# Seven block products for pair 10 and for six more second units, with the conditioning laid out anew

## The chip, the cores and the metric

One core of a Trainium2 chip runs the whole program in one launch. The metric is device time in microseconds (us), the median of several runs. A profiled execution has its own time, and a span from its first to its last instruction.

## The reference, cut to what matters

Two transformer blocks in float32 on 512 tokens of width 1024. Between the mixers stand five gated feed-forward networks, called network 0 to 4 here (four of hidden width 2816 in the first block, one of 2816 in the second):

```
def _swiglu(h, w_in, w_out):
    a, b = jnp.split(h @ w_in, 2, axis=-1)
    return (jax.nn.silu(a) * b) @ w_out

x = x + 0.5 * _swiglu(_rmsnorm(x, ffn_norm[layer, 0]), ffn_w_in[layer, 0], ffn_w_out[layer, 0])
...
x = x + g2 * swiglu(modulate(rms_norm(x, norm2_gain[layer]), sh2, sc2), w_ffn_in[layer], w_ffn_out[layer])
...
mod = jax.nn.silu(c) @ w_ada[layer] + b_ada[layer]
```

The last line, the conditioning, is a product of one vector (two with the context's) with a 1024 x 6144 matrix. The second block needs its result, the kernel computes it on VectorE beside networks 0, 1 and 2.

## The kernel before, in words

**Units.** All large weights come in units of 128 x 2048 float32 (1 MB): 256 output features of 1024 inputs. SyncE loads unit after unit into two buffers by turns (RAW), each load released by the low part of the unit two before. ScalarE rounds the block to its high part (WH, `split`, L604), as soon as the unit two before, which used the same buffer, is done on TensorE. VectorE takes the low part (WL = RAW - WH, L1456). A plain unit is 8 x 2 x 3 matmuls of 512 columns (high by high, high by low, low by high; `three`, L2603 to L2605).

**A network.** 22 input units in 11 pairs (pair i is units 2i and 2i+1), then 12 output units in four groups of three (8, 8 and 6 of the 22 hidden rows, so the third unit has 36 matmuls). The first unit of a pair gives the gate part, which is scaled by the norm (RINV; networks 0 to 3, called late in the code) and goes through silu on ScalarE; the second gives the factor, and `gated` (L1732, L1736) multiplies both into GF. `high_g` on ScalarE (L819) and `low_g` on VectorE (L1811) split GF into GHI and GLO, on which the output units work. GHI lies on the memory of the token sums TH and TL and of the weight sums SH and SL.

**Seven products.** In the pairs listed in SEVEN the first unit, and in those in SEVEN_B the second too, is computed by a Strassen-like scheme: the 2 x 2 blocks of weights and tokens are combined so that seven block products of 12 matmuls of 256 columns each do for eight. For it VectorE makes four sums of weight blocks in RAW (`raw_sums`, L1760 to L1770), ScalarE their high parts (L792), VectorE their low parts (`sums_low`, L1777); after the unit VectorE joins the seven results from PSUM (`joined`, L1794 to L1799 for a first unit, L1791 to L1799 for a second) with one result that ScalarE copied out (`first_product`, L812). `scaled_seven` (L1806) is the scaling. On TensorE `seven` waits for `q_raw` and, as a first unit, for `a_ready` (network 4: `silu_ready`) of the pair before, as a second for `g_mul`; its third, fourth and fifth products wait for the low parts of one sum each, the sixth for `w_lo`.

**Order by hand.** VectorE's order in pair i of `ffn_seven`, networks 0 to 2, is: gating of pair i-1; the low part of unit 2i+1 (or sums and their low parts, if by seven); joining of unit 2i; raw sums of unit 2i+2; scaling of pair i; low sums of unit 2i+2; half a conditioning block, if ADA_IN has the pair. In network 0 the low parts of the token sums (L1752) stand in pair 2, ahead of the low sums. Each engine takes its work in this order.

**Conditioning.** 24 blocks, 8 per network, each in two halves of 512 KB that GpSimd loads into one buffer (ADAW). A half is eight operations of 128 x 256 on VectorE (L1612, L1615), an odd one is followed by a transpose into PSUM and a reduction (L1621, L1623; bank 7 in the pairs, bank 3 in the output units). ADA_IN gives the halves per pair (before and after the low sums), ADA_OUT those per output unit, where `beside(c)` places them behind the low part of unit c+1. Of the 16 halves 8 stand in pairs 2 to 9 and 8 in output units 1, 2, 4, 5, 7, 8, 9 and 10.

**The end of the input.** Pair 10 is plain in all networks; GHI is written from unit 19's end on (`visit_done` >= u0 + 20), three pairs of GLO ahead of unit 20's scaling, four behind it.

```
def conditioned(count, bank):
...
                if i in SEVEN[n]:
                    joined(i)
                else:
                    scaled(i)
                if i + 1 in SEVEN[n]:
                    raw_sums(i + 1)
```

Of the kernel before, what the change touches and what calls it, by code (L numbers as in the profile page):

```python
# [42 lines left out]
FFN_IN, FFN_OUT = 22, 12  # L43
# [92 lines left out]

N_LATE = 6

SEVEN = {0: range(3, 10), 1: range(2, 10), 2: range(2, 10), 3: range(2, 10), 4: range(2, 10)}

SEVEN_B = {3: (3, 5, 7, 9), 4: (2, 3, 5, 6, 8, 9)}

ADA_IN = {2: (0, 1), 3: (0, 1), 4: (0, 1), 5: (0, 1), 6: (0, 1), 7: (0, 1), 8: (0, 1), 9: (0, 1)}
ADA_OUT = {1: 1, 2: 1, 4: 1, 5: 1, 7: 1, 8: 1, 9: 1, 10: 1}

ONCE_DVE = ("zeros", "fold_ready", "mlb_in", "c_ready", "c_lo", "mod_ready", "ml_rows", "ml_bl")
ONCE_ACT = ("cond_ready", "fx_const", "c_hi", "sb_const", "crms", "ml_bh")
# [5 lines left out]
def build(nc, A):  # L153
    ctx = ExitStack()
    with ctx:
# [441 lines left out]
        def _(act):  # L597
# [171 lines left out]
            def ffn_seven(n, shift=None, lead=None, rest=None, aside=None):  # L769
                u0, m_, name = U_FFN[n], N_NORM[FFN_NORM[n]], FFN_NORM[n]  # L770
                late = m_ < N_LATE

                def silu(i):
                    if not late and i in SEVEN[n]:
                        act.wait_ge(*q_posts(n, i, 4))
                    elif not late:
                        act.wait_ge(T["g_mul"].sem, 22 * n + 2 * i)
                        act.wait_ge(T["visit_done"].sem, u0 + 2 * i + 1)
                    for m in range(2):
                        if late:  # L780
                            act.wait_ge(T["a_ready"].sem, 22 * n + 2 * i + m + 1)
                        x = SIL7 if i in SEVEN[n] else SIL
                        act.activation(x[:, m, :], x[:, m, :] if late or i in SEVEN[n] else PS[:, m, :], ACT.Silu).then_inc(*T["silu_ready"].up())

                def sums_high(i, s=0):

                    u, before = u0 + 2 * i + s, units_upto(n, i, s)
                    for q in range(4):
                        act.wait_ge(*q_sums(n, i, q, s))
                        if before and q < 3:  # L790
                            act.wait_ge(T["q_prod"].sem, 4 * before - 2 + q)
                        act.activation(sum_high(u, q), sum_raw(u, q), ACT.Copy).then_inc(*T["q_hi"].up())  # L792

                def tokens_whole():

                    for t in range(KT):
                        last = act.activation(HG[:, t, :], XT[:, t, :], ACT.Copy, scale=gain_of(name, t))
                    last.then_inc(*T["q_hi"].up())

                def tokens_high(t0, t1):  # L800

                    for t in range(t0, t1):
                        act.wait_ge(T["q_sum"].sem, q_sums(n, SEVEN[n][0], t - 4)[1])
                        act.activation(TH[:, t, :, :], TF[:, t, :, :], ACT.Copy).then_inc(*T["q_hi"].up())

                def first_product(i, s=0):

                    before = units_upto(n, i, s)
                    act.wait_ge(*q_prods(n, i, 0, s))
                    if before:  # L810
                        act.wait_ge(T["q_post"].sem, 4 * before - 3)
                    act.activation(WB[:, 0, :] if s else WK[:, 0, :], PS[:, first_bank(s), 0:SC], ACT.Copy).then_inc(*T["q_copy"].up())  # L812

                def high_g(p0, p1):
                    for p in range(p0, p1):
                        act.wait_ge(T["g_mul"].sem, 22 * n + 2 * p + 2)
                        if p == 0:
                            act.wait_ge(T["visit_done"].sem, u0 + 20)
                        act.activation(GHI[:, 2 * p:2 * p + 2, :], GF[:, 2 * p:2 * p + 2, :], ACT.Copy).then_inc(*T["gh_ready"].up())  # L819

                def beside(c):
                    if c == 0:
                        high_g(8, 11)
                    if aside:
                        aside(c)

                if not late:
                    first_parts(n, shift)
                    T["q_hi"].up()
                elif lead:  # L830
                    lead()
                    split(u0 + 2)
                else:
                    split(u0 + 1)
                if late and not lead:
                    tokens_whole()
                if late:
                    inverse(m_)
                if rest:
                    rest()  # L840
                if not lead:
                    split(u0 + 2)
                silu(0)
                if not lead:
                    tokens_high(0, 4)
                for i in range(1, FFN_IN // 2):
                    split(u0 + 2 * i + 1)
                    if lead and i == 1:
                        tokens_whole()
                    if i in SEVEN[n]:  # L850
                        first_product(i)
                    if i in SEVEN_B.get(n, ()):
                        sums_high(i, 1)
                    if i == FFN_IN // 2 - 1:
                        high_g(0, 4)
                    split(u0 + 2 * i + 2)
                    if i in SEVEN_B.get(n, ()):
                        first_product(i, 1)
                    if not late:
                        silu(i)  # L860
                    if i + 1 in SEVEN[n]:
                        sums_high(i + 1)
                    if late:
                        silu(i)
                    if lead and i == 1:
                        tokens_high(0, 4)
                high_g(4, 8)
                residual(RES[f"ffn{n}"], u0 + FFN_IN, 3, False, ("mix0", "ffn2", "mix1", None, None)[n], beside)

            def residual(r, u0, chunks, loop, then=None, aside=None, ahead=0):  # L870
# [580 lines left out]
        def _(dve):  # L1451
# [248 lines left out]
            def ffn_seven(n, gain=None, shift=None, scale=0.5, lead=None, rest=None, aside=None):  # L1700
# [113 lines left out]
                carries = n < N_ADA // ADA_PER  # L1814
                taken = [2 * ADA_PER * n]

                def conditioned(count, bank):

                    for j in range(carries * count):
                        u, h = taken[0] // 2, taken[0] % 2  # L1820
                        conditioning(u, h)
                        if h:
                            if bank < 4:
                                dve.wait_ge(T["g_mul"].sem, 22 * n + 22)
                            turned_sums(u - ADA_PER * n + 1, ADA_PER * n - 1, bank)
                        taken[0] += 1

                def beside(c):
                    if c < 2:
                        low_g(7 + 3 * c, 10 + c)  # L1830
                    conditioned(ADA_OUT.get(c, 0), 3)
                    if carries and c == 11:
                        modulation(n, 3)
                    if aside:
                        aside(c)
# [18 lines left out]
                for i in range(1, FFN_IN // 2):  # L1854
                    gated(i - 1)
                    if i in SEVEN_B.get(n, ()):
                        raw_sums(i, 1)
                        sums_low(i, 1)
                    else:
                        split(u0 + 2 * i + 1)  # L1860
                    if i == 1 and not lead:
                        token_lows(0, 4)
                    if i == FFN_IN // 2 - 1:
                        low_g(0, 3)
                    conditioned(ADA_IN.get(i, (0, 0))[0], 7)
                    if i in SEVEN[n]:
                        joined(i)
                    else:
                        scaled(i)
                    if i + 1 in SEVEN[n]:  # L1870
                        raw_sums(i + 1)
                    if i in SEVEN[n]:
                        scaled_seven(i)
                    if i == 2 and lead:
                        token_lows(0, 4)
                    if i + 1 in SEVEN[n]:
                        sums_low(i + 1)
                    else:
                        split(u0 + 2 * i + 2)
                    if i == 1 and lead:  # L1880
                        token_sums()
                    conditioned(ADA_IN.get(i, (0, 0))[1], 7)
                low_g(3, 7)
                gated(FFN_IN // 2 - 1)
                residual(RES[f"ffn{n}"], u0 + FFN_IN, 3, False, scale, ("mix0", "ffn2", "mix1", None, None)[n], beside)

            def residual(r, u0, chunks, loop, scale, then=None, aside=None, ahead=0):
# [712 lines left out]
        def _(pe):  # L2600
# [193 lines left out]
            def ffn_seven(n, aside=None):  # L2794
# [9 lines left out]
                for i in range(FFN_IN // 2):  # L2804
                    for s in range(2):
# [14 lines left out]
                        feature_major(u % 2, HH, HL, (2 * s, 2 * s + 1), ready=8 * m_ if i + s == 0 else None).then_inc(*T["visit_done"].up())  # L2820
                        if i + s == 0:
                            norm(m_)
                residual(RES[f"ffn{n}"], u0 + FFN_IN, FFN_CHUNKS, GHI, GLO, False, 22 * n, aside=beside)
                if carries:
                    pe.wait_ge(T["ada_mod"].sem, n + 1)
# [660 lines left out]
```

## Time and profile before

| | |
|---|---|
| median of 3 runs | 2769.15 us (2769.1 to 2770.93) |
| profiled execution | 2770.69 us |
| its span | 2769.0 us |
| TensorE busy | 2748.1 us, 99% |
| VectorE busy | 1859.5 us, 67% |
| ScalarE busy | 1168.3 us, 42% |
| granted TensorE clock, mean | 0.998 |

Busy time of TensorE is the time with a matmul under way; matmuls overlap in the records, so the mean of one (389 ns for 512 columns) is more than its share of the time. The clock is of full speed, 2.4 GHz, through all stages with which the change has to do. In timeline rows the first number is a start in us from the span's begin, the second the time to the end of the last instruction merged into the row.

### The profile page before, as it was taken

Reading aid. Unit: us, or ns where it says so; the run is one execution under the profiler, and the core shown is the slowest. Engines: PE = TensorE matmul, PEld = TensorE weight load, DVE = VectorE, ACT = ScalarE, POOL = GpSimd, SP = SyncE. Lnnn points to the kernel's source line nnn. Section 1 sums busy time; section 2 is a strip of 40 time slices with the busy share of each in tenths; the row PEclk is TensorE's granted clock in tenths of the full one; section 3 lists DMA queues with packets and bytes.
Section 4 is the critical chain, followed back from the end, with each engine's and each line's share of the span. In section 5 each row is a group of like instructions: output and inputs, shape, how many; then the busy total and the mean of one; then the engine's idle time right before and its main releaser. Section 6 shows DMA issues by size and latency. Waiting matters only on the chain. (4 is left out here: it accounts for less than half of the span.)

```text
span 2769.0 us, 37283 instructions
## 1 busy us (share of the span) xinstructions
PE 2748.1 (99%) x15352; PEld 2367.4 (85%) x15352; DVE 1859.5 (67%) x2563; ACT 1168.3 (42%) x1406; POOL 39.3 (1%) x77
## 2 busy tenths in 40 slices
PE   9999999999999999999999999999999999999998
PEld 7898887789988899888877899888898988899988
DVE  6997666468885688865665688835555543688743
ACT  5333237453342433423555544424443432444422
POOL 0000000000000000000000000000000000000000
PEclk9999999999999999999999999999999999999999
DMA  4333441123334333334111233224321122223332
GB/s 163 114 131 129 134 139 63 46 99 122 124 120 145 129 108 123 129 134 127 59 49 61 107 107 108 102 97 157 109 80 67 47 77 100 71 103 107 107 107 76
DMA packets 69106, 289.22 MB, mean 104 GB/s; under 512 B 7680, under 2 KB 30336, under 8 KB 40528
## 3 DMA queue, kind: packets, MB, share of 16 engines
q1 hardware_dynamic: 60480, 257.18, 26.9%
q0 software_dynamic: 8032, 29.37, 3.3%
q8 instruction: 121, 1.98, 0.3%
q10 hardware_dynamic: 432, 0.36, 0.0%
q14 instruction: 41, 0.34, 0.0%
HBM read 284.78 MB, written 2.10 MB: 104 GB/s over the span
## 5 line engine op out<-in xcount | busy, mean ns | idle before, releaser
L604 ACT ACTIVATE sb_WH<-sb_RAW 128x2048 fp32r<-128x2048 f32 x238 | 455.5, 1914 | 783.0 <-PE PS L2605 780.0
L2603 PE MATMUL PS<-sb_HH,sb_WH 128*128 128x512 f32 (+1 forms) x2100 | 757.8, 361 | 5.2 <-DVE sb_WL L1456 1.8
L2604 PE MATMUL PS<-sb_HL,sb_WH 128*128 128x512 f32 (+1 forms) x2100 | 751.8, 358 | 0.0
L2605 PE MATMUL PS<-sb_HH,sb_WL 128*128 128x512 f32 (+1 forms) x2100 | 751.5, 358 | 0.0
L1456 DVE TENSOR_TENSOR sb_WL<-sb_RAW,sb_WH 128x2048 fp32r<-128x2048 f32 x190 | 434.7, 2288 | 347.7 <-ACT sb_WH L604 347.7
L2603 PEld LDWEIGHTS PS<-sb_HH,sb_WH 128*128 128x128 f32 x2100 | 396.7, 189 | 69.5 <-issue 3.3
L2604 PEld LDWEIGHTS PS<-sb_HL,sb_WH 128*128 128x128 f32 x2100 | 396.9, 189 | 58.2 <-issue 1.4
L2605 PEld LDWEIGHTS PS<-sb_HH,sb_WL 128*128 128x128 f32 x2100 | 396.6, 189 | 58.4
L2603 PE MATMUL PS<-glh_GHI,sb_WH 128*128 128x512 f32 (+1 forms) x924 | 350.8, 380 | 0.0
L2605 PE MATMUL PS<-glh_GHI,sb_WL 128*128 128x512 f32 (+1 forms) x924 | 350.2, 379 | 0.0
L2604 PE MATMUL PS<-glh_GLO,sb_WH 128*128 128x512 f32 (+1 forms) x924 | 350.1, 379 | 0.0
L2605 PEld LDWEIGHTS PS<-glh_GHI,sb_WL 128*128 128x128 f32 x924 | 173.8, 188 | 32.8
L2603 PEld LDWEIGHTS PS<-glh_GHI,sb_WH 128*128 128x128 f32 x924 | 173.8, 188 | 32.7
L2604 PEld LDWEIGHTS PS<-glh_GLO,sb_WH 128*128 128x128 f32 x924 | 173.8, 188 | 32.6
L2603 PE MATMUL PS<-sv_TH,sv_SH 128*128 128x256 f32 x588 | 166.4, 283 | 0.0
L2604 PE MATMUL PS<-sv_TL,sv_SH 128*128 128x256 f32 x588 | 166.4, 283 | 0.0
L2605 PE MATMUL PS<-sv_TH,sv_SL 128*128 128x256 f32 x588 | 166.4, 283 | 0.0
L792 ACT ACTIVATE sv_SH<-sb_RAW 128x512 fp32r<-128x512 f32 x147 | 93.1, 634 | 155.0 <-DVE sb_RAW L1763 130.2
L1615 DVE SCALAR_TENSOR_TENSOR ff_ACC<-ff_ADAW,sb_CS,ff_ACC 128x256 f32<-128x256 f32 x336 | 137.1, 479 | 2.8 <-DMA ff_ADAW<-in_w_ada 2.8
L2603 PE MATMUL PS<-sb_WH,sb_HH 128*128 128x256 f32 x448 | 132.2, 295 | 0.0
L2604 PE MATMUL PS<-sb_WL,sb_HH 128*128 128x256 f32 x448 | 127.0, 284 | 0.0
L2605 PE MATMUL PS<-sb_WH,sb_HL 128*128 128x256 f32 x448 | 127.0, 284 | 0.0
(455 smaller groups left out, 4011.7 us busy)
## 6 DMA issues: line engine op xcount, KB each, us to landing
sb_RAW<-in_weights SPq DMA_DIRECT2D x221, 1024.0 KB, 4.9
ff_ADAW<-in_w_ada POOLq DMA_DIRECT2D x48, 512.0 KB, 3.9
sb_RAW<-in_weights SPq DMA_DIRECT2D x39, 512.0 KB, 5.0
out_t<-sb_XT SPq DMA_DIRECT2D x8, 256.0 KB, 2.4
sb_XT<-in_x SPq DMA_DIRECT2D x3, 512.0 KB, 8.5
sb_RAW<-in_weights SPq DMA_DIRECT2D x4, 256.0 KB, 3.5
b_CT<-in_ctx POOLq DMA_DIRECT2D x1, 1024.0 KB, 7.2
hy_BD<-in_c_gates POOLq DMA_DIRECT2D x1, 512.0 KB, 3.5
```

Source lines behind the costliest of these rows:

```text
L604: act.activation(WH[slot][:, :], RAW[slot][:, :], ACT.Copy).then_inc(*T["w_hi"].up())
L792: act.activation(sum_high(u, q), sum_raw(u, q), ACT.Copy).then_inc(*T["q_hi"].up())
L1456: dve.tensor_tensor(WL[slot][:, :], RAW[slot][:, :], f32(WH[slot][:, :]), ALU.subtract).then_inc(*T["w_lo"].up())
L1615: ins = dve.scalar_tensor_tensor(ACC[:, j, :], w, c, ACC[:, j, :], ALU.mult, ALU.add)
L2603: pe.matmul(out, wh, xh, start=start, stop=False)
L2604: pe.matmul(out, wh, xl, start=False, stop=False)
L2605: return pe.matmul(out, wl, xh, start=False, stop=stop)
```

## The change

Pair 10 goes into SEVEN in all five networks. Pairs 3 and 7 of networks 0, 1 and 2 go into SEVEN_B. Conditioning leaves pairs 3 and 7 and joins output units 3 and 6. As pair 10's products read the token sums, GHI is written from unit 20's end on; all eight high parts of pairs 0 to 7 follow one another on ScalarE behind unit 22's, four of their low parts stand on VectorE between the low part of unit 22 and pair 10's scaling and four behind it. Gating of pair 10 moves behind the low part of output unit 1. TensorE waits ahead of the output units for pair 10's joining, since they write its banks.

```diff
-SEVEN = {0: range(3, 10), 1: range(2, 10), 2: range(2, 10), 3: range(2, 10), 4: range(2, 10)}
-
-SEVEN_B = {3: (3, 5, 7, 9), 4: (2, 3, 5, 6, 8, 9)}
-
-ADA_IN = {2: (0, 1), 3: (0, 1), 4: (0, 1), 5: (0, 1), 6: (0, 1), 7: (0, 1), 8: (0, 1), 9: (0, 1)}
-ADA_OUT = {1: 1, 2: 1, 4: 1, 5: 1, 7: 1, 8: 1, 9: 1, 10: 1}
+SEVEN = {0: range(3, 11), 1: range(2, 11), 2: range(2, 11), 3: range(2, 11), 4: range(2, 11)}
+
+SEVEN_B = {0: (3, 7), 1: (3, 7), 2: (3, 7), 3: (3, 5, 7, 9), 4: (2, 3, 5, 6, 8, 9)}
+
+ADA_IN = {2: (0, 1), 4: (0, 1), 5: (0, 1), 6: (0, 1), 8: (0, 1), 9: (0, 1)}
+ADA_OUT = {1: 1, 2: 1, 3: 1, 4: 1, 5: 1, 6: 1, 7: 1, 8: 1, 9: 1, 10: 1}
...
                         if p == 0:
-                            act.wait_ge(T["visit_done"].sem, u0 + 20)
+                            act.wait_ge(T["visit_done"].sem, u0 + 21)
...
-                    if i == FFN_IN // 2 - 1:
-                        high_g(0, 4)
                     split(u0 + 2 * i + 2)
                     if i in SEVEN_B.get(n, ()):
                         first_product(i, 1)
+                    if i == FFN_IN // 2 - 1:
+                        high_g(0, 8)
...
-                high_g(4, 8)
                 residual(RES[f"ffn{n}"], u0 + FFN_IN, 3, False, ("mix0", "ffn2", "mix1", None, None)[n], beside)
...
-                def conditioned(count, bank):
+                def conditioned(count, bank, done):
...
                         if h:
-                            if bank < 4:
-                                dve.wait_ge(T["g_mul"].sem, 22 * n + 22)
+                            dve.wait_ge(T["g_mul"].sem, 22 * n + 2 * done)
                             turned_sums(u - ADA_PER * n + 1, ADA_PER * n - 1, bank)
...
                 def beside(c):
-                    if c < 2:
-                        low_g(7 + 3 * c, 10 + c)
-                    conditioned(ADA_OUT.get(c, 0), 3)
+                    if c == 0:
+                        gated(FFN_IN // 2 - 1)
+                        low_g(8, 10)
+                    elif c == 1:
+                        low_g(10, 11)
+                    conditioned(ADA_OUT.get(c, 0), 3, 11)
...
-                    if i == FFN_IN // 2 - 1:
-                        low_g(0, 3)
-                    conditioned(ADA_IN.get(i, (0, 0))[0], 7)
+                    conditioned(ADA_IN.get(i, (0, 0))[0], 7, i)
                     if i in SEVEN[n]:
                         joined(i)
                     else:
                         scaled(i)
                     if i + 1 in SEVEN[n]:
                         raw_sums(i + 1)
+                    if i == FFN_IN // 2 - 1:
+                        split(u0 + 2 * i + 2)
+                        low_g(0, 4)
                     if i in SEVEN[n]:
                         scaled_seven(i)
...
                     if i + 1 in SEVEN[n]:
                         sums_low(i + 1)
-                    else:
+                    elif i < FFN_IN // 2 - 1:
                         split(u0 + 2 * i + 2)
...
-                    conditioned(ADA_IN.get(i, (0, 0))[1], 7)
-                low_g(3, 7)
-                gated(FFN_IN // 2 - 1)
+                    conditioned(ADA_IN.get(i, (0, 0))[1], 7, i)
+                low_g(4, 8)
...
+                pe.wait_ge(*q_posts(n, FFN_IN // 2 - 1, 4))
                 residual(RES[f"ffn{n}"], u0 + FFN_IN, FFN_CHUNKS, GHI, GLO, False, 22 * n, aside=beside)
```

## Rows read from the trace of the kernel before

**Rows 1.** The page, busy us, share of the span and instructions of each engine.
```profile
PE 2748.1 (99%) x15352; PEld 2367.4 (85%) x15352; DVE 1859.5 (67%) x2563; ACT 1168.3 (42%) x1406; POOL 39.3 (1%) x77
```

**Rows 2.** Timeline of ScalarE, network 0, units 18 to 21: start, us, engine, line.
```profile
202.47 1.91 ACT L604 ACTIVATE sb_WH<-sb_RAW 128x2048 fp32r<-128x2048 f32 x1 [1.52 <-PE PS L2605]
...
212.54 1.92 ACT L604 ACTIVATE sb_WH<-sb_RAW 128x2048 fp32r<-128x2048 f32 x1 [7.89 <-PE PS L2605]
...
223.45 1.92 ACT L604 ACTIVATE sb_WH<-sb_RAW 128x2048 fp32r<-128x2048 f32 x1 [5.92 <-PE PS L2605]
225.27 3.89 ACT L819 ACTIVATE glh_GHI<-gf_GF 128x1024 fp32r<-128x1024 f32 x4
234.33 1.92 ACT L604 ACTIVATE sb_WH<-sb_RAW 128x2048 fp32r<-128x2048 f32 x1 [5.17 <-PE PS L2605]
```

**Rows 3.** Timeline of ScalarE, network 0, ends of units 5, 6 and 7.
```profile
75.88 1.92 ACT L604 ACTIVATE sb_WH<-sb_RAW 128x2048 fp32r<-128x2048 f32 x1 [2.54 <-PE PS L2605]
...
85.95 1.92 ACT L604 ACTIVATE sb_WH<-sb_RAW 128x2048 fp32r<-128x2048 f32 x1 [7.89 <-PE PS L2605]
...
97.57 1.92 ACT L604 ACTIVATE sb_WH<-sb_RAW 128x2048 fp32r<-128x2048 f32 x1 [2.03 <-PE PS L2605]
```

**Rows 4.** Timeline of TensorE, network 0, first matmul of unit 7.
```profile
86.30 0.50 PE L2603 MATMUL PS<-sb_HH,sb_WH 128*128 128x512 f32 x1 [0.44 <-DVE sb_WL L1456]
```

**Rows 5.** Timeline of VectorE, network 1, pairs 2 and 3.
```profile
645.71 0.61 DVE L1612 TENSOR_SCALAR ff_ACC<-ff_ADAW,sb_CS 128x256 f32<-128x256 f32 x2
...
648.61 1.28 DVE L1732 TENSOR_TENSOR gf_GF<-PS,sb_RINV 128x512 f32<-128x512 f32 x2
...
656.16 0.69 DVE L1794 TENSOR_TENSOR wk_WK<-PS,wk_WK 128x512 f32<-128x512 f32 x1 [2.71 <-PE PS L2605]
...
658.55 0.68 DVE L1760 TENSOR_TENSOR sb_WL<-sb_RAW,sb_WH 128x512 fp32r<-128x512 f32 x1
...
663.14 1.22 DVE L1806 TENSOR_TENSOR wk_WK<-wk_WK,sb_RINV 128x1024 f32<-128x1024 f32 x1
...
666.68 3.25 DVE L1615 SCALAR_TENSOR_TENSOR ff_ACC<-ff_ADAW,sb_CS,ff_ACC 128x256 f32<-128x256 f32 x8
...
671.34 1.28 DVE L1732 TENSOR_TENSOR gf_GF<-PS,sb_RINV 128x512 f32<-128x512 f32 x2
...
673.89 2.29 DVE L1456 TENSOR_TENSOR sb_WL<-sb_RAW,sb_WH 128x2048 fp32r<-128x2048 f32 x1
```

**Rows 6.** Timeline of VectorE, network 3, pair 9, both units by seven.
```profile
1741.72 0.68 DVE L1760 TENSOR_TENSOR sb_WL<-sb_RAW,sb_WH 128x512 fp32r<-128x512 f32 x1
...
1746.31 1.89 DVE L1777 TENSOR_TENSOR sv_SL<-sb_RAW,sv_SH 128x512 fp32r<-128x512 f32 x3
1748.12 0.69 DVE L1777 TENSOR_TENSOR sb_WL<-sb_RAW,sb_WH 128x512 fp32r<-128x512 f32 x1
1749.29 0.69 DVE L1794 TENSOR_TENSOR wk_WK<-PS,wk_WK 128x512 f32<-128x512 f32 x1 [0.49 <-issue]
...
1759.37 0.42 DVE L1791 TENSOR_TENSOR gf_GF<-PS,gw_WB 128x256 f32<-128x256 f32 x1 [4.07 <-issue]
...
1764.51 2.29 DVE L1456 TENSOR_TENSOR sb_WL<-sb_RAW,sb_WH 128x2048 fp32r<-128x2048 f32 x1
```

**Rows 7.** Timeline of VectorE, network 0: pair 3, end of the input, output units.
```profile
81.40 1.28 DVE L1732 TENSOR_TENSOR gf_GF<-PS,sb_RINV 128x512 f32<-128x512 f32 x2
...
83.96 2.28 DVE L1456 TENSOR_TENSOR sb_WL<-sb_RAW,sb_WH 128x2048 fp32r<-128x2048 f32 x1
...
238.49 4.62 DVE L1811 TENSOR_TENSOR glh_GLO<-gf_GF,glh_GHI 128x1024 fp32r<-128x1024 f32 x4
...
281.72 2.29 DVE L1456 TENSOR_TENSOR sb_WL<-sb_RAW,sb_WH 128x2048 fp32r<-128x2048 f32 x1 [0.64 <-ACT sb_WH L604]
```

**Rows 8.** The page, DMA issues: KB each, median us from issue to landing.
```profile
sb_RAW<-in_weights SPq DMA_DIRECT2D x221, 1024.0 KB, 4.9
```

## The prediction

> **What bounds the kernel now.** I read the page's busy shares first, then the timelines of the three engines round the pairs that change. TensorE is busy 99% of the span, VectorE 67% [rows 1]. So time can only be won by giving TensorE less to do, and lost where it waits. The profiled execution took 2770.69 us for a span of 2769.0; the median of the runs is 2769.15. I make the sum as a difference, check it against the profiled execution, and put it on the median.
>
> ScalarE's high-part copy of a weight block (L604) starts when the unit two before it in use order is done, 0.08 us after that unit's last matmul. The distance between two such starts is therefore a unit's time [rows 2]: 202.47 to 212.54, 10.07 us for a unit of seven products (unit 18 of network 0); 212.54 to 223.45, 10.91 us for the plain unit after it; 223.45 to 234.33, 10.88 us for a plain unit after a plain one. There is no wait in any of them.
>
> **The gross gain.** A seven-product unit is 84 matmuls of 256 columns, 10.07/84 = 120 ns each; a plain one 48 of 512, 10.88/48 = 227 ns each. In columns seven products are one eighth fewer, in time 0.8 us.
> - Pair 10, first unit, networks 0 to 2: 10.88 becomes 10.07, and the plain unit behind it 10.91 for 10.88: 0.78 us each. Networks 3 and 4: the unit already follows a seven-product one, 10.91 + 10.88 becomes 10.08 + 10.91: 0.80 each. In all 3 x 0.78 + 2 x 0.80 = 3.94 us.
> - Second units of pairs 3 and 7, networks 0 to 2: 10.91 becomes 10.08 (network 3's unit 19, of this kind, ran from 1749.29 to 1759.37, the starts of the joinings before and behind it [rows 6]): 0.83 each, six of them, 4.98 us.
> Gross: 8.92 us. The Trainium skill ("TensorE: Matmul & The Clock Gate", section "Wait — 56ns, not 53.3ns?") gives a warm matmul N/2.4 GHz plus about 2.5 ns, 109 and 216 ns here; an estimate from that page is 84 x 109.2 = 9.17 against 48 x 215.8 = 10.36 us, 1.19 saved per unit, and the gross would be 13 us. The trace's spacing is wider by 11 ns for either length, which costs the form with more instructions; the sum goes by the rows.
>
> **What VectorE must do for it.** VectorE takes its work in order, so I walk it. Steps, from start to next start:
> - a half of the conditioning: even 645.71 to 648.61, 2.90 us; odd, with transpose and reduction, 666.68 to 671.34, 4.66 [rows 5];
> - gating a plain pair: 671.34 to 673.89, 2.55 [rows 5]; low part of a plain block: 2.2;
> - sums and low parts of a second unit's seven products: 1741.72 to 1748.72 (last start 1748.12 plus 0.60), 7.0; the first low sum is finished 5.28 after their start [rows 6];
> - joining a first unit, the next unit's raw sums, and scaling by the norm (L1806), after which TensorE may start the next pair: 656.16 to 663.14 + 1.22, 8.20. With the low sums 656.16 to 666.68, 10.52 [rows 5];
> - gating a pair whose second unit was by seven: 1759.37 to 1764.51, 5.14 [rows 6].
> The first unit of a pair waits at its start for that scaling (a_ready). Today the joining starts when the first unit is done, and scaling is over 8.2 us later, inside the second unit's 10.9. In network 3 it is inside 10.08, since there no conditioning stands ahead.
>
> **Pair 7, networks 0 to 2.** Zero is the end of unit 13 (pair 6's second). The last low sum of unit 14 leaves VectorE at -0.31 (666.68 against a unit end at 656.09 + 10.91 = 667.00 in the like place). Pair 6 still carries a half, and after the change it is an odd one: in pairs 2, 4, 5, 6, 8, 9 the halves go even, odd, even, odd, even, odd. So: conditioning to 4.35, gating of pair 6 to 6.90, sums and lows of unit 15 to 13.90. Unit 14 has been done since 10.07, and only now its joining starts: 3.8 us late. The scaling is over at 13.90 + 8.20 = 22.10, while TensorE is through with unit 15 at 20.15. It waits 1.95, and a restart costs more: in network 0 today unit 7 takes 97.57 - 85.95 = 11.62 for 10.91 us [rows 3], though its block (83.96 + 2.28 = 86.24 [rows 7]) is only 0.37 after the unit before (85.87); the other 0.34 is refilling, with the first matmul at 86.30 [rows 4]. So 1.95 + 0.34 = 2.29 us lost per network, 6.87 in three, against 2.49 won there.
>
> Unit 15 itself does not wait: its first low sum is ready at 6.90 + 5.28 = 12.18, wanted two products after 10.07, at 12.95.
>
> **Pair 3, networks 1 and 2.** Pair 2 carries an even half: it ends 648.61 - 646.02 = 2.59 after the end of unit 5 (656.09 less 10.07) [rows 5], gating at 5.15, sums at 12.15, scaling at 20.35. Late by 0.20 + 0.34 = 0.54 each, 1.08 for both.
>
> **Pair 3, network 0.** Pair 2 is late already: the token lows stand in it, and conditioning ends only at 81.40, 5.60 after the end of unit 5 (75.80), gating at 83.96, 8.16 after it [rows 3, 7]. First low sum of unit 7 at 13.44, wanted 12.95: 0.49 + 0.34 = 0.83. Unit 7 ends at 20.98. The sums end at 15.16, scaling at 23.36: 2.38 + 0.34 = 2.72. The stall of 0.71 that stands there today goes. Net of that 2.84.
>
> **Pair 10.** With unit 20 by seven, the high gated parts, which lie on the token sums, can start only after unit 20, one unit later than today; one plain unit (10.91) covers them. From unit 20's end: joining 656.16 to 658.55, 2.39 [rows 5], the low part of block 22 to 4.6 (its high part is ready at about 2.0), four low gated parts 4.62 [rows 7], done at 9.3 (4.6 + 4.62, less a step's overlap of 0.1 and rounding, 9.2 to 9.3); their high parts are out of ScalarE at 1.9 + 3.89 = 5.8 [rows 2]. The first output unit wants them at 10.91, or 10.57 with the refill. 1.3 us are to spare, and the new wait on pair 10's joining (2.5) is long over. Priced at nothing. The next four pairs, behind another scaling (1.14) at about 15.1, have until 21.8; pair 10's gating goes ahead of the second output unit and the third wants it ten us later. VectorE is free when unit 20 ends, also in networks 3 and 4 (gating 5.14 plus a split 2.2 in a unit of 10.08).
>
> **Conditioning in ten output units.** Two halves move from pairs 3 and 7 to output units 3 and 6. They stand behind a block's low part: block 26's is over at 281.72 + 2.29 = 284.0 [rows 7], 1.9 before unit 25's end (unit 20's end 234.25 + 4 x 10.88 + one of 36 matmuls, 8.16 = 285.9). The next block's high part comes 2.0 after that end. An even half (output unit 3) ends 1.0 after the end, an odd one (output unit 6) 2.8, so one low part comes 0.8 late, and it had 10.88 - 4.3 = 6.6 to spare. GpSimd's two transfers move along with them, in a stretch where a weight block of 1 MB lands in 4.9 us [rows 8] and has a whole unit to do so. Nothing. SyncE's loads are released by low parts that come up to 5 us late in the stalled pairs; landing 4.9 later they still meet their unit's end.
>
> **Sum.** -8.92 + 6.87 + 1.08 + 2.84 = **+1.87 us**: per network +2.69, +0.39, +0.39, -0.80, -0.80. On the profiled execution 2772.6, on the median 2771.0. By the rate of the Trainium skill's page ("TensorE: Matmul & The Clock Gate") alone it would be 11 x 0.39 = 4.3 us less, an estimate that the trace's spacing does not bear out.
>
> **Bounds.** Seven waits carry a refill of 0.34; were it nothing the sum is -0.5. After each stall unit 9 or 17 has its block only about 0.2 us before the refill would show: joining at 13.90, low sums over at 24.42, gating 29.56, block 31.9, unit 16's end 32.5. If that tips, up to 0.3 in each of six places, +3.7 in all. So 2768.6 to 2772.9, and the runs of before alone spread 1.8 us: 2767.5 to 2774.5.
>
> **Rivals.**
> - All covered: VectorE's lateness is absorbed and the gross gain stays, 2760.2 us. For it: network 3 has such pairs, 3 and 7 among them, and in the one of [rows 6] the units follow at 10.08. Against: there nothing of 2.9 to 4.7 us stands ahead of the gating, and in the walk 13.90 against 10.07 is far outside reading error. It decides where the joining comes less than 1.5 us late. 7%.
> - Slower: the turn from pair 10 to the output units stalls. Place: the first output unit's wait for gated parts. If it in fact waits until all eight are out, 15.1 - 10.9 + 0.34 = 4.5 us in each of five networks, 2771.0 + 22.5 = 2793.5. It decides when the fourth low part is later than 10.57, against 9.3 walked. For it: today the same parts have two units. Against: today four of them take 4.62 with ScalarE ahead throughout. 5%.
>
> **Chances.** This kernel's measurement tells about 0.2%, 5.5 us, from no change. My forecast, 88%, lies within that: VectorE gives back what TensorE saves. Faster by more 7%, slower by more 5%.
>
> **What would show it.** Right: the high-part copies of network 1 show pair 7's first unit (14) to unit 16 as 10.07, 10.08 and 12.4; a PE idle of about 2 us before the next pair with VectorE's L1806 as its releaser, three of them plus one in network 0's pair 3; L1794 of pair 7 starting right behind L1777 and not behind TensorE; networks 3 and 4 0.8 us shorter each; output unit 0 starting without idle. Wrong: units 8 and 16 starting without a wait, or idle ahead of the first GHI matmul.

## The result, and the profile after

The changed kernel takes **2774.50 us** (median of 23 runs), the kernel before 2770.37 (median of 23). The ratio is 1.0018, 95% interval [1.0013, 1.0024]: 0.18% slower, more than the noise of so many runs, and just inside the 0.2% that I had called no change. The first three runs of before gave 2769.15; I had put the sum on that. The execution profiled together with this result ran at a mean granted clock of 0.85 throughout and took 2991.39 us, so it can't be laid beside the profile of before; all rows of the changed kernel in this section come from run e1, whose profiled execution took 2774.99 us, span 2773.3 us.

Its page, the first lines; they answer to [rows 1]:

```profile
span 2773.3 us, 38374 instructions
...
PE 2743.0 (99%) x15748; PEld 2381.6 (86%) x15748; DVE 1934.9 (70%) x2702; ACT 1199.5 (43%) x1461; POOL 39.4 (1%) x77
```

TensorE is busy 5.1 us less than before (2743.0 against 2748.1), and the span is 4.3 us longer. So its idle time grew by some 9 us. VectorE has 75 us more work. Where the idle time stands, the view of TensorE's waits says (which instruction waited, for whose result; us in total, times, longest us). Changed kernel:

```profile
PE PS L2604 <- DVE wk_WK L1805: 9.8, 6, 2.5
PE PS L2604 <- DVE sb_WL L1455: 2.3, 4, 1.2
PE PS L3271 <- DVE mk_KEYS L2417: 2.1, 1, 2.1
```

Kernel before:

```profile
PE PS L2603 <- DVE sb_WL L1456: 2.7, 5, 1.2
PE PS L3269 <- DVE mk_KEYS L2416: 2.1, 1, 2.1
```

The changed kernel's code stands up to two lines away (L1805 is L1806 of before, L1455 is L1456, L1731 is L1732, L1793 is L1794, L1810 is L1811). One line is new: six waits, 9.8 us, all for the scaling of pair 3 or 7. They stand at the start of units 8 and 16 of networks 0, 1 and 2. The other rows of the list stay within 0.4 us of what they were.

The last row of both lists is the same wait, 2.1 us, between networks 3 and 4, far from the change. It matters for the account below: in the kernel before, the granted clock fell to half just behind it. TensorE's timeline and the view of windows (bounds, length, busy us and instructions of each engine, granted clock, DMA), kernel before:

```profile
2132.36 1.01 PE L3269 MATMUL PS<-b_CMV,mk_KEYS 128*128 128x129 f32 x3 [2.10 <-DVE mk_KEYS L2416]
```

```profile
2132.36:2135.76 3.40, 3.40 (x16) 3.40 (x17) 0.34 (x2) 0.39 (x1) 0.00 (x0) 0.50 0.84 263
```

Pair 7 of network 1 in the changed kernel, VectorE's timeline (start, us, engine, line):

```profile
738.91 1.28 DVE L1731 TENSOR_TENSOR gf_GF<-PS,sb_RINV 128x512 f32<-128x512 f32 x2
...
741.46 0.69 DVE L1759 TENSOR_TENSOR sb_WL<-sb_RAW,sb_WH 128x512 fp32r<-128x512 f32 x1
...
748.46 0.69 DVE L1793 TENSOR_TENSOR wk_WK<-PS,wk_WK 128x512 f32<-128x512 f32 x1
...
755.43 1.22 DVE L1805 TENSOR_TENSOR wk_WK<-wk_WK,sb_RINV 128x1024 f32<-128x1024 f32 x1
```

and TensorE's at the same place:

```profile
754.35 0.28 PE L2606 MATMUL PS<-sv_TH,sb_WL 128*128 128x256 f32 x1
756.79 0.36 PE L2604 MATMUL PS<-sb_HH,sb_WH 128*128 128x256 f32 x1 [2.17 <-DVE wk_WK L1805]
```

Unit 15 ends with the first of the two (754.35 + 0.28 = 754.63); its start is 10.08 earlier and unit 13's end another 10.08, at 734.47. From there gating starts at 4.44 (walked: 4.35), the sums at 6.99 (6.90), the joining at 13.99 (13.90), and the scaling is over at 22.18 (22.10). The joining has no idle in front: VectorE ran straight into it from the low sums, while its like in [rows 5] stands behind 2.71 us of idle. TensorE's first matmul of unit 16 follows at 756.79.

### The profile page after: what moved, and what is told of

The parts are those of the page before. It is cut to its first block and busy times, and to the rows that moved or that the text cites. A ratio compares the mean times of both kernels' runs of the same rounds, so it can differ in the third digit from the quotient of the medians.

```text
span 2989.7 us, 38374 instructions
## 1 busy us (share of the span) xinstructions
PE 2972.3 (99%) x15748; PEld 2459.8 (82%) x15748; DVE 1937.2 (65%) x2702; ACT 1200.1 (40%) x1461; POOL 39.3 (1%) x77
## 5 line engine op out<-in xcount | busy, mean ns | idle before, releaser
L1455 DVE TENSOR_TENSOR sb_WL<-sb_RAW,sb_WH 128x2048 fp32r<-128x2048 f32 x179 | 409.5, 2288 | 379.2 <-ACT sb_WH L604 379.2
L2604 PE MATMUL PS<-glh_GHI,sb_WH 128*128 128x512 f32 (+1 forms) x924 | 374.7, 406 | 0.0
L2605 PE MATMUL PS<-glh_GLO,sb_WH 128*128 128x512 f32 (+1 forms) x924 | 374.2, 405 | 0.0
L2606 PE MATMUL PS<-glh_GHI,sb_WL 128*128 128x512 f32 (+1 forms) x924 | 373.9, 405 | 0.0
L2605 PE MATMUL PS<-sv_TL,sv_SH 128*128 128x256 f32 x720 | 209.6, 291 | 0.0
L2606 PE MATMUL PS<-sv_TH,sv_SL 128*128 128x256 f32 x720 | 209.3, 291 | 0.0
L2604 PE MATMUL PS<-sv_TH,sv_SH 128*128 128x256 f32 x720 | 209.2, 291 | 0.0
L2605 PEld LDWEIGHTS PS<-sv_TL,sv_SH 128*128 128x128 f32 x720 | 143.2, 199 | 0.0
L2606 PEld LDWEIGHTS PS<-sv_TH,sv_SL 128*128 128x128 f32 x720 | 143.0, 199 | 0.0
L2604 PEld LDWEIGHTS PS<-sv_TH,sv_SH 128*128 128x128 f32 x720 | 143.0, 199 | 0.0
```

The costliest lines, as they stand in the source:

```text
L1455: dve.tensor_tensor(WL[slot][:, :], RAW[slot][:, :], f32(WH[slot][:, :]), ALU.subtract).then_inc(*T["w_lo"].up())
L2604: pe.matmul(out, wh, xh, start=start, stop=False)
L2605: pe.matmul(out, wh, xl, start=False, stop=False)
L2606: return pe.matmul(out, wl, xh, start=False, stop=stop)
```

## Experiments

All are edits of the changed kernel, measured beside the kernel before. Unit times in the text are differences between the ends of units.

### e1: the changed kernel again

No edit.

> The changed kernel once more, for an undisturbed profile; nothing is changed in it. Theory A (VectorE's lateness in pairs 3 and 7 of networks 0 to 2, as in the prediction): units 16 of networks 0 to 2 take about 12.4 us, unit 8 of network 0 about 12.8, units 8 of networks 1 and 2 about 10.6, the turn to output units waits nowhere, span of before plus 1.9 us. Theory B (the missing 2 us are in the turn from pair 10 to the output units): an idle of 0.4 us or more ahead of the first matmul on GHI in each network. Theory C (stalls as in A, but the granted clock dips behind them): a stretch at half clock of some 3.4 us in this run that before does not have, each costing 1.7 us.

Measured: 2774.47 us, median of 11 (2772.86 to 2777.15), before 2770.16; 1.0017 [1.0008, 1.0026]. Unit 16 takes 12.49, 12.48 and 12.47 us in networks 0, 1 and 2; unit 8 takes 10.67 and 10.65 in networks 1 and 2. The second units of pairs 3 and 7 take 10.08, pair 10's first 10.07 or 10.08. Only unit 8 of network 0 stands out: 14.34 us instead of 12.8. The view of windows, the last number but two being the granted clock; the first stretch lies behind that wait, the second holds the wait of unit 16, the third lies behind it:

```profile
99.98:103.38 3.40, 3.40 (x18) 3.40 (x17) 3.33 (x8) 2.93 (x4) 0.00 (x0) 0.50 0.29 39
184.00:187.00 3.00, 0.82 (x8) 0.65 (x7) 2.97 (x4) 2.23 (x4) 0.00 (x0) 1.00 0.00 0
187.20:190.60 3.40, 3.40 (x31) 3.40 (x30) 3.33 (x7) 2.71 (x3) 0.00 (x0) 1.00 0.15 29
```

Before the first stretch TensorE was idle for 2.55 us (unit 8 of network 0), and then got 1.2 GHz for 3.4 us: 18 matmuls in the time in which 31 ran in the third stretch. What such a stretch costs is read from the same unit with and without it: 13.96 and 13.98 us in e7 for 12.49 and 12.47 here (units 16 of networks 0 and 2), so 1.5 us. Unit 8 without it would take 12.8, as walked (an estimate, 14.34 less 1.5). A half-clock stretch at 2137.7 us is in before's profile too (at 2132.4) and isn't new.

So Theory A holds for the waits and Theory C for what stands behind one of them.

The turn to the output units is as walked. Changed kernel, network 0, VectorE and then TensorE's first matmul on GHI:

```profile
243.63 4.62 DVE L1810 TENSOR_TENSOR glh_GLO<-gf_GF,glh_GHI 128x1024 fp32r<-128x1024 f32 x4
```

```profile
249.69 0.39 PE L2604 MATMUL PS<-glh_GHI,sb_WH 128*128 128x512 f32 x1
```

The four low parts are over at 248.25, 9.3 us after unit 20's end (238.97), and the matmul has no idle in front. Theory B falls.

### e2 and e3: without the six second units

```diff
# e2 and e3
-SEVEN_B = {0: (3, 7), 1: (3, 7), 2: (3, 7), 3: (3, 5, 7, 9), 4: (2, 3, 5, 6, 8, 9)}
+SEVEN_B = {3: (3, 5, 7, 9), 4: (2, 3, 5, 6, 8, 9)}
# e2 alone
-ADA_IN = {2: (0, 1), 4: (0, 1), 5: (0, 1), 6: (0, 1), 8: (0, 1), 9: (0, 1)}
+ADA_IN = {2: (0, 1), 3: (0, 1), 4: (0, 1), 5: (0, 1), 6: (0, 1), 7: (0, 1), 8: (0, 1), 9: (0, 1)}
-ADA_OUT = {1: 1, 2: 1, 3: 1, 4: 1, 5: 1, 6: 1, 7: 1, 8: 1, 9: 1, 10: 1}
+ADA_OUT = {1: 1, 2: 1, 4: 1, 5: 1, 7: 1, 8: 1, 9: 1, 10: 1}
```

> Only pair 10 by seven products with its new order; SEVEN_B, ADA_IN and ADA_OUT as before. Theory A: -3.9 us against the kernel before (3 x 0.78 + 2 x 0.80), 0.9986 of it. Theory B: above -3.9 by what the turn loses, -1.9 if all of the missing time is there.

> The changed kernel with SEVEN_B as before (no second units in networks 0 to 2), but the conditioning in six pairs and ten output units. Theory A: same time as the run with pair 10 alone, within 0.5 us. If the ten output units cost something of their own, it is the difference between the two: a rival (theory D) has up to 2 us here.

Measured: e2 2765.06 us (11 runs, 2764.91 to 2766.60), 0.9985 [0.9976, 0.9994]; e3 2765.02 (2764.79 to 2766.70), 0.9984 [0.9975, 0.9993]. The lowest run lies 3.7 below the lowest of before (2768.59), and in e2's trace the last unit ends 4.2 us earlier. Pair 10 brings its 3.9 us, and the ten output units cost nothing. Whatever was lost, the six second units lost: from e2's trace to e1's, pairs 3 and 7 of networks 0 to 2 grow by 7.8 us (1.5 of it the half clock), where the matmuls of the six units are 5.0 us shorter. The medians are further apart, 9.4 us, because they come from runs with different numbers of half-clock stretches.

That can be seen here. The runs of e2 lie at 2764.9 to 2765.1 and at 2766.5 to 2766.6; its profiled execution, 2766.48 us, has the stretch behind the wait for mk_KEYS. The profiled execution of e3, 2765.12 us, has the same wait, 2.1 us, and full clock behind it:

```profile
2129.10:2132.50 3.40, 3.40 (x29) 3.40 (x30) 0.33 (x2) 0.39 (x1) 0.00 (x0) 1.00 0.81 258
```

The unit in which it stands takes 28.90 us in e2 and 27.39 in e3, and 28.97 in the kernel before.

### e4: the scaling ahead of the raw sums

```diff
+                    if i in SEVEN[n] and i < FFN_IN // 2 - 1:
+                        scaled_seven(i)
                     if i + 1 in SEVEN[n]:
                         raw_sums(i + 1)
                     if i == FFN_IN // 2 - 1:
                         split(u0 + 2 * i + 2)
                         low_g(0, 4)
-                    if i in SEVEN[n]:
                         scaled_seven(i)
```

> The changed kernel with the scaling of pair i (which releases the next first unit) ahead of the raw sums of pair i+1 instead of behind them, in pairs 0 to 9. Theory A says that VectorE's work as a whole is late, not this one step: units 16 lose their wait of 2.3 us, units 17 get one of 2.0, units 9 of network 0 2.0, and the sum falls by only 1.9 us against the changed kernel. A rival, that only the release is late: all stalls of units 8 and 16 go, -9 us against the changed kernel.

Measured: 2772.97 us (11 runs), 1.0011 [1.0002, 1.0020]; 1.5 below the changed kernel. The wait moved as walked. Unit 16 falls to 10.52 us, and unit 17, plain, rises from 10.91 to 12.87; network 0's unit 9 rises to 12.86, and units 9 of networks 1 and 2 to 11.5. In the view of waits:

```profile
PE PS L2605 <- DVE sb_WL L1455: 9.6, 10, 1.7
```

against 2.3 us, 4 times in the changed kernel, and the line with L1805 is gone. What waits changes; that TensorE waits for VectorE doesn't. The profiled execution has no half-clock stretch behind these waits. Its last unit ends 1.4 us before e1's, which has one more such stretch (1.5 us). So the 1.5 us in the medians is the size of one stretch, and the 1.9 that I had expected from the waits themselves didn't come.

### e5: conditioning ahead of no second unit, twelve halves in the output units

```diff
-ADA_IN = {2: (0, 1), 4: (0, 1), 5: (0, 1), 6: (0, 1), 8: (0, 1), 9: (0, 1)}
-ADA_OUT = {1: 1, 2: 1, 3: 1, 4: 1, 5: 1, 6: 1, 7: 1, 8: 1, 9: 1, 10: 1}
+ADA_IN = {4: (0, 1), 5: (0, 1), 8: (0, 1), 9: (0, 1)}
+ADA_OUT = {0: 1, 1: 1, 2: 1, 3: 1, 4: 2, 5: 1, 6: 1, 7: 1, 8: 1, 9: 1, 10: 1}
```

> The changed kernel with the conditioning out of pairs 2 and 6 too: four halves in pairs 4, 5, 8 and 9, twelve in the output units (one each in 0 to 10, two in 4). Theory A (conditioning ahead of the gating in front of a second unit by seven makes VectorE late): no wait at units 16, none at units 8 of networks 1 and 2, about 0.6 us left at unit 8 of network 0 (token lows in pair 2), every granted-clock dip behind them gone; 9.0 us below the kernel before, about 2761, ratio 0.9967. Theory D (second units by seven cannot be fed in networks 0 to 2 however the conditioning lies): waits of 2 us or more stay at units 16 or 17, the time stays above 2768.

Measured: 2766.00 us (11 runs, 2764.68 to 2767.34), 0.9986 [0.9977, 0.9995]: 5 us more than expected. The waits in the pairs went as expected (units 16: 10.08; unit 8 of networks 1 and 2: 10.08, of network 0 10.75). New ones came in output units 6 and 7 (units 28 and 29), 0.6 to 1.3 us each, six in all, 4.8 us. VectorE's timeline, network 0:

```profile
295.97 3.25 DVE L1614 SCALAR_TENSOR_TENSOR ff_ACC<-ff_ADAW,sb_CS,ff_ACC 128x256 f32<-128x256 f32 x8 [4.50 <-DMA ff_ADAW<-in_w_ada]
...
303.77 0.62 DVE L1611 TENSOR_SCALAR ff_ACC<-ff_ADAW,sb_CS 128x256 f32<-128x256 f32 x2 [0.79 <-DMA ff_ADAW<-in_w_ada]
```

There is one buffer for the conditioning weights. The second half in one output unit waits 4.50 us for its transfer, and all that stands behind it on VectorE, the block's low part too, waits along. I had counted VectorE's work there, not its waiting.

### e6: pair 6's half alone moved out

```diff
-ADA_IN = {2: (0, 1), 4: (0, 1), 5: (0, 1), 6: (0, 1), 8: (0, 1), 9: (0, 1)}
-ADA_OUT = {1: 1, 2: 1, 3: 1, 4: 1, 5: 1, 6: 1, 7: 1, 8: 1, 9: 1, 10: 1}
+ADA_IN = {2: (0, 1), 4: (0, 1), 5: (0, 1), 8: (0, 1), 9: (0, 1)}
+ADA_OUT = {0: 1, 1: 1, 2: 1, 3: 1, 4: 1, 5: 1, 6: 1, 7: 1, 8: 1, 9: 1, 10: 1}
```

> The changed kernel with pair 6's half alone moved out (to output unit 0); pair 2's stays. Theory A: the three waits of 2.4 us at units 16 go, the 0.6 of units 8 in networks 1 and 2 and the 2.7 of network 0 stay; 7.2 us below the changed kernel, about 2767.3, less 1.5 for each clock dip that hung on a wait at units 16. If the length of the half counts and not its place: no more than 1.8 us each.

Measured: 2767.30 us (11 runs), 0.9991 [0.9982, 1.0000]; 7.2 us below the changed kernel. The three units 16 fall by 2.41, 2.40 and 2.39 us to 10.08 and nothing else moves. One half of conditioning, 4.66 us of VectorE at one place of each network, was worth the wait of 2.4.

### e7: network 0's pair 3 as before

```diff
-SEVEN_B = {0: (3, 7), 1:
+SEVEN_B = {0: (7,), 1:
```

> The changed kernel with network 0's pair 3 as before (second unit plain), all else unchanged. In the undisturbed profile that unit 8 took 4.27 us more than before, 2.70 by the walk of VectorE's work and 1.6 by a granted clock of half speed just behind the wait. Theory C (the clock dip hangs on the two waits standing close together there): unit 7 back to 11.6, unit 8 to 10.07, no dip at 100 us, 3.5 us below the changed kernel, about 2771.0. Rival (dips come by chance or elsewhere, as many as before): only 2.0 us below, 2772.5.

Measured: 2772.78 us (11 runs, 2770.31 to 2773.69), 1.0009 [1.0000, 1.0018]. Units 7 and 8 are back at 11.64 and 10.07, and no half clock stands at 100 us. But units 16 of networks 0 and 2 now take 13.96 and 13.98 us. The window behind the first:

```profile
184.10:187.50 3.40, 3.40 (x18) 3.40 (x18) 3.33 (x7) 2.38 (x3) 0.00 (x0) 0.50 0.23 43
```

The same wait that ended at full clock in e1 ended at half clock here. The profiled execution (2773.64 us) has full clock behind the wait at 2137 us, so it has two half-clock stretches like e1, at other waits. The rival's 2772.5 is what came, and Theory C in the form given here, that the fall hangs on two waits close together, is wrong.

### e8: a half in pair 10

```diff
-ADA_IN = {2: (0, 1), 4: (0, 1), 5: (0, 1), 6: (0, 1), 8: (0, 1), 9: (0, 1)}
-ADA_OUT = {1: 1, 2: 1, 3: 1, 4: 1, 5: 1, 6: 1, 7: 1, 8: 1, 9: 1, 10: 1}
+ADA_IN = {4: (0, 1), 5: (0, 1), 8: (0, 1), 9: (0, 1), 10: (1, 0)}
+ADA_OUT = {0: 1, 1: 1, 2: 1, 3: 1, 4: 1, 5: 1, 6: 1, 7: 1, 8: 1, 9: 1, 10: 1}
```

> The changed kernel with the conditioning ahead of no second unit by seven and no two halves in one output unit: one half each in pairs 4, 5, 8, 9 and (ahead of the joining) 10, and in output units 0 to 10. Theory A: as in the run with four and twelve halves, waits at units 8 and 16 gone but for 0.6 at unit 8 of network 0, and its waits of 0.6 to 1.3 us at output units 28 and 29, where the second half waited for its transfer, gone too (4.8 us): 9 us below the kernel before, lowest runs near 2760.0, ratio 0.9967. Theory D2 (twelve or eleven halves are too many for the output units anyhow): waits at output units stay and the ratio is above 0.998.

Measured: 2764.68 us (11 runs), 0.9981 [0.9972, 0.9990]. The waits of e5 are gone, others came: 0.82 us at each unit 22, 0.4 to 0.7 at units 26. Network 0, VectorE:

```profile
234.01 0.68 DVE L1793 TENSOR_TENSOR wk_WK<-PS,wk_WK 128x512 f32<-128x512 f32 x1
...
272.00 3.26 DVE L1614 SCALAR_TENSOR_TENSOR ff_ACC<-ff_ADAW,sb_CS,ff_ACC 128x256 f32<-128x256 f32 x8 [2.17 <-DMA ff_ADAW<-in_w_ada]
```

Unit 20 ended at 232.0, and the joining starts 2.0 late, behind the half. The walked 9.3 becomes 11.3 against the 10.57 at which TensorE needs the four low parts: 0.7 over, and 0.8 was measured. That also tests the spare time in the prediction's pair 10: it was 1.3 us and no more. The wait of unit 26 comes from another transfer that had too little time (2.17 us).

### e9: the changed kernel a third time

No edit.

> The changed kernel a third time, nothing changed in it, for the clock behind its waits. Theory C: the waits of units 8 and 16 last as long as in the second look (2.7 and 2.3 to 2.4 us net of clock), since they come from VectorE's order of work; the half-clock stretches of 3.4 us behind them need not stand at the same ones. If the dips were a fixed cost of the wait at unit 8 of network 0, exactly that one would have one again and the others none.

Measured: one run, 2774.92 us. All units as in e1 within 0.04 us, with the half clock at 99.7 us behind the wait of unit 8 of network 0 (14.36 us) and behind none of the other five of these waits; the one behind the wait for mk_KEYS is there too, at 2137.5.

### e10: the half of pair 2 in pair 1

```diff
-ADA_IN = {2: (0, 1), 4: (0, 1), 5: (0, 1), 6: (0, 1), 8: (0, 1), 9: (0, 1)}
-ADA_OUT = {1: 1, 2: 1, 3: 1, 4: 1, 5: 1, 6: 1, 7: 1, 8: 1, 9: 1, 10: 1}
+ADA_IN = {1: (0, 1), 4: (0, 1), 5: (0, 1), 8: (0, 1), 9: (0, 1)}
+ADA_OUT = {0: 1, 1: 1, 2: 1, 3: 1, 4: 1, 5: 1, 6: 1, 7: 1, 8: 1, 9: 1, 10: 1}
```

> The changed kernel with conditioning halves in pairs 1, 4, 5, 8 and 9 and in output units 0 to 10: as in the run with pair 6's half moved out, but pair 2's half stands in pair 1, behind which VectorE had 5 to 6 us idle. Theory A: no wait at units 16 nor at units 8 of networks 1 and 2, 0.6 us left at unit 8 of network 0, none at output units 22 and 26 (pair 10's half, which made the joining 2 us late, is gone); 8.9 less 0.7 plus network 0's old wait gone, in all 9 us below the kernel before, lowest runs near 2760, ratio 0.9967. Theory D2: output units wait all the same and the ratio is above 0.998.

Measured: **2761.30 us** (6 runs, 2760.19 to 2762.19), 0.9969 [0.9957, 0.9981]. It beats the kernel before by 8 us and the changed one by 13. Unit ends by ScalarE's timeline, network 1, pair 7:

```profile
747.05 1.92 ACT L604 ACTIVATE sb_WH<-sb_RAW 128x2048 fp32r<-128x2048 f32 x1 [0.69 <-PE PS L2606]
...
757.13 1.92 ACT L604 ACTIVATE sb_WH<-sb_RAW 128x2048 fp32r<-128x2048 f32 x1 [7.90 <-PE PS L2606]
```

10.08 us for unit 16, which took 12.48. Of the six waits one is left, 0.68 us at unit 8 of network 0. The last unit ends 8.7 us earlier than before, both traces with one half-clock stretch; the gross gain was 8.92.

## Why the prediction was wrong

It said no change, 2771.0 us, 2767.5 to 2774.5. The measured 2774.50 lies at the very edge, and the interval of the ratio excludes 1. That it touches the range at all is luck: the walk's own bounds ended at 2772.9, and the rest was the spread of before's runs, which came from something else (below). By its steps:

- **The gross gain, 8.92 us: right.** Second units 10.08 for 10.91, pair 10 10.07 or 10.08 with 10.91 behind; e10's trace ends 8.7 earlier.
- **Pair 7, 2.29 us lost each: right.** 2.42, 2.41, 2.40, with VectorE's walk off by 0.1 us over 22 us. e6 shows the cause by taking away the half that stood ahead.
- **Pair 3 of networks 1 and 2, 0.54 each: right,** 0.59 and 0.58.
- **Pair 3 of network 0: the waits right, the cost not.** Unit 7 went from 11.62 to 10.89 (walked: 10.9). Unit 8 was to take 10.07 + 2.72 = 12.8 and took 14.34. The 1.5 over are the half clock.
- **Pair 10 priced at nothing: right** (e1, e2), and e8 shows that the spare time was real and small.
- **Ten output units priced at nothing: right** (e3).
- **Rivals.** "All covered" was ruled out, and e10 shows what it needs. "The turn stalls" was ruled out by e1.

The step that failed is the sum, which says that the three groups of waits and nothing else stand against the gain, and with it the bounds. What a wait costs was taken from the one stall that before had there, 0.71 us long, with a refill of 0.34. The changed kernel has four waits of more than 2 us, and behind such waits the granted clock can fall to half for 3.4 us. Its cost, 1.5 us a time, had no term and no bound. The trace of before held a case, though outside the stretches that change: the wait of 2.10 us at 2132 us with the half clock behind it. I had not looked into it.

Account, between the two traces, whose last units end 4.3 us apart: the walk's +1.87 came out as +2.4 in the networks' units (+2.9 in network 0 without the clock, +0.57, +0.54, -0.80, -0.80); one half clock more is 1.5; and unit 0 ends 0.4 later in e1, which is not the change's: in the eleven traces (all but the one at 0.85) it ends anywhere from 20.2 to 21.2 us.

The runs that were not profiled bear this out, since each has its mean granted clock on record. Of the 22 runs of the changed kernel beside the one at 0.85, the five at 0.999 took 2772.9 to 2773.5 us, the nine at 0.998 took 2774.3 to 2775.0, the eight at 0.997 took 2775.8 to 2777.8, with no exception. Both profiled executions of the middle group (e1, e9) have two half-clock stretches; by an estimate (half of 3.41 us in 2773) one stretch more or less changes the mean by 0.0006. The kernel before has two groups as well, 2768.6 to 2769.2 and 2770.3 to 2770.9, and its profiled execution, from the upper one, has one stretch. So the 2769.15 on which I put the sum, the middle one of three runs, is by this reading a run without any, and the usual run of the changed kernel has two: 2771.0 + 0.5 (the units' 2.4 for 1.87) + 2 x 1.5 = 2774.5. The spread of 1.8 us that I added to the bounds was one such stretch.

Not settled: what decides behind which wait the clock falls. A count of stretches for a run that was not profiled is argued from its time and mean clock, not seen.

## What to carry to other kernels

When one engine is full and a change unloads it by loading another, walk the other engine's queue past the change in order, from rows of like places: here that gave what each wait took, at full clock, to within 0.15 us, and showed that what matters is which work stands ahead of the step that releases the full engine, not the helper's mean load (70%). Helper work with no deadline goes where the helper is idle; two halves of it moved turned 0.2% slower into 0.3% faster. And a work item with its own single buffer can't be put twice in a row, since its transfer then holds up everything behind it.

## What the runs showed of the hardware

A wait of TensorE may cost more than its length. Four profiled executions had waits of 2.17 to 2.55 us in these pairs (e1, e6, e7, e9), twelve waits in all. Behind five of them the granted clock was 0.50 (1.2 GHz) for 3.41 us: behind the wait of unit 8 of network 0 in three of three (e1, e6, e9), behind that of a unit 16 in two of nine (both in e7; none in e1 or e9). The wait of 2.10 us for mk_KEYS stands in all eleven executions, the kernel before among them, and had such a stretch behind it in eight, all but e3, e7 and e8. Each stretch began between 0.1 us before and 1.3 us after the first matmul behind the wait, and cost 1.5 to 1.6 us where the same unit is on record with and without it. The four longest waits of e4 in the pairs, 1.7 us each, had none behind them. The Trainium skill ("TensorE: Matmul & The Clock Gate", section "HAM oscillation — how this bites in real kernels") describes matmuls that start slow behind each wait for data, because the clock was throttled during it. The traces agree in kind (0.50, 3.41 us each time); but here it came behind 13 of 23 waits of 2.1 to 2.6 us and not behind the others of the same length, and what decides between them no run showed.
